# A four-layer fp32 block on one core: SBUF tensors placed on multiples of 256 bytes, the delta rule's gate columns used as weights, and its output's products with the state grouped

## What is computed

```python
beta = jax.nn.sigmoid(dn_b)                       # dn_b, dn_a: 4 + 4 columns of h @ w_in
g = -jnp.exp(dn_A_log) * jax.nn.softplus(dn_a + dn_dt_bias)
...
def step(state, inp):                             # 4 chunks of 64 tokens, 4 heads
    u_c, w_c, a_c, qd_c, kt_c, dl_c = inp
    v_new = u_c - jnp.einsum('bhck,bhkv->bhcv', w_c, state)
    o = jnp.einsum('bhck,bhkv->bhcv', qd_c, state) + jnp.einsum('bhcj,bhjv->bhcv', a_c, v_new)
    state = state * dl_c[..., None, None] + jnp.einsum('bhck,bhcv->bhkv', kt_c, v_new)
    return state, o
```

## Time and profile before

| | |
|---|---|
| median of the runs | 1903.18 us |
| lowest and highest | 1902.38, 1908.37 us |
| the profiled execution | 1908.99 us, its span 1907.2 us |
| TensorE's mean granted clock | 0.993 |
| busy: TensorE, VectorE, ScalarE, GpSimd | 99%, 65%, 50%, 16% of the span |

### The profile page before, as it was taken

How to read it: one execution, slowest core, us unless ns; L and a number is a source line. 1 busy time by engine, 2 the same in 40 slices (tenths; PEclk the granted TensorE clock), 3 DMA queues, 4 the chain that set the end, 5 groups by cost and what they waited for, 6 DMA issues and landing times.

```text
span 1907.2 us, 36402 instructions
## 1 busy us (share of the span) xinstructions
PE 1879.3 (99%) x15460; PEld 1791.1 (94%) x15460; DVE 1246.2 (65%) x1678; ACT 955.7 (50%) x1381; POOL 308.5 (16%) x176
## 2 busy tenths in 40 slices
PE   7999999999999999999999999999999999999998
PEld 7989998998899999999989999999999899999998
DVE  6884567665689545877658775577547684677643
ACT  5633456544563435564445445555534444556533
POOL 0050231000003203200002342320001352321000
PEclk9999999999999999999999999999999999999999
DMA  6443344655445323555565553355555663345553
GB/s 228 161 145 111 120 146 159 211 187 198 145 154 178 110 97 127 200 181 182 193 209 184 178 179 131 123 188 193 187 186 179 211 195 121 132 167 188 190 187 100
DMA packets 92161, 317.59 MB, mean 167 GB/s; under 512 B 11744, under 2 KB 12896, under 8 KB 91744
## 3 DMA queue, kind: packets, MB, share of 16 engines
q1 hardware_dynamic: 91424, 314.69, 48.9%
q10 hardware_dynamic: 576, 0.57, 0.1%
HBM read 304.99 MB, written 1.05 MB: 160 GB/s over the span
## 4 chain that ended last, share of the span: by engine, by line
PE 90%; DVE 7%; ACT 1%; DMA 1%; issue 1%; SPq 0%; DVEq 0%; ACTq 0%
PE bank L2001 89%; DVE wlo L1126 3%; DVE area L1126 2%; PE bank L2543 1%; DVE area L1132 1%; DMA raw<-in_weights 1%; DVE hl L1132 1%; DVE xT L1132 1%; ACT area L630 1%; ACT whi L636 0%; PE bank L2561 0%; PE bank L2220 0%; DVE area L1196 0%; DVE xT L1126 0%; DVE area L1645 0%
## 5 line engine op out<-in xcount | busy, mean ns | idle before, releaser
L1126 DVE TENSOR_TENSOR wlo<-raw,whi 128x1024 fp32r<-128x1024 f32 x518 | 659.9, 1289 | 399.1 <-ACT whi L636 398.6
L2001 PE MATMUL bank<-hh,whi 128*128 128x256 f32 x2928 | 835.3, 286 | 15.8 <-DVE wlo L1126 13.1
L2001 PE MATMUL bank<-hh,wlo 128*128 128x256 f32 x2928 | 818.6, 281 | 0.0
L2001 PE MATMUL bank<-hl,whi 128*128 128x256 f32 x2928 | 811.7, 281 | 0.0
L636 ACT CAST whi<-raw 128x1024 fp32r<-128x1024 f32 x572 | 589.0, 1046 | 412.3 <-PE bank L2001 361.2
L2001 PEld LDWEIGHTS bank<-hh,whi 128*128 128x128 f32 x2928 | 555.7, 190 | 30.0 <-DVE wlo L1126 14.7
L2001 PEld LDWEIGHTS bank<-hl,whi 128*128 128x128 f32 x2928 | 555.8, 191 | 1.9 <-issue 1.9
L2001 PEld LDWEIGHTS bank<-hh,wlo 128*128 128x128 f32 x2928 | 556.2, 190 | 0.0
L1781 POOL TENSOR_TENSOR area<-area 128x512 f32<-128x512 f32 (+4 forms) x86 | 137.4, 1604 | 559.3 <-ACT area L630 219.4
L1781 POOL TENSOR_TENSOR wlo<-raw,whi 128x1024 fp32r<-128x1024 f32 x54 | 134.0, 2483 | 426.3 <-ACT whi L636 426.3
L2001 PE MATMUL bank<-area 64*64 64x64 f32 (+7 forms) x1928 | 184.9, 268 | 0.7 <-DVE area L1196 0.7
(11 more groups left out here) (129 smaller groups left out, 1915.5 us busy)
## 6 DMA issues: line engine op xcount, KB each, us to landing
raw<-in_weights SPq DMA_DIRECT2D x572, 512.0 KB, 4.1
area<-area SPq DMA_DIRECT2D x96, 64.0 KB, 3.5
area<-area SPq DMA_DIRECT2D x16, 128.0 KB, 3.8
cst<-in_const SPq DMA_DIRECT2D x1, 1188.0 KB, 7.3
cst<-in_const SPq DMA_DIRECT2D x1, 1024.5 KB, 5.5
xT<-in_x SPq DMA_DIRECT2D x4, 256.0 KB, 8.0
out<-xT SPq DMA_DIRECT2D x4, 256.0 KB, 2.9
area<-in_lev SPq DMA_DIRECT2D x2, 384.0 KB, 6.6
```

Source lines behind the costliest of these rows:

```text
L1126: return v.tensor_tensor(dst, x, y, op)
L2001: return e.matmul(ps, x, y, start=start, stop=stop, skip_group_check=skip)
```

## The change

It does three things. It allocates hh, hl, RSB, the region of area, SW and cst in that order right after wlo, so that each starts on a multiple of 256 bytes; par, small and RST come last. It computes the gate columns with SW as weights (16 or 8 columns) and hh, hl as the moving operand, into 16 rows of a bank, one step earlier; VectorE copies these rows to ABR, and two fp32 matmuls with ABR as weights and a stacked 16 x 8 identity (8 new columns of `small`) as moving operand transpose them and add the high and the low half. ScalarE's cast of SW and VectorE's subtraction move to after the second step of qkv, ahead of the third; the bank of the result is freed by "ab". And the four products with the state are issued ahead of the four with v_new, the first of each bank with the start flag.

```diff
@@ -56,7 +56,7 @@
                          ("dnout", 1), ("retout", 4), ("pscale", 4), ("alog", 8), ("dtb", 8)])
 N_PAR2 = _columns(PAR2, [("attn", 8), ("mlp", 8), ("final", 8), ("idxk", 1), ("sinks", 8)])
 N_PAR = DEPTH * (N_PAR1 + N_PAR2)
-N_SMALL = 64 + 512
+N_SMALL = 64 + 512 + 8
 
 
 class Job:
@@ -319,17 +319,19 @@
         raw = sb("raw", [P, RAW, 1024])
         whi = sb("whi", [P, RING, 1024], F32R)
         wlo = sb("wlo", [P, RING, 1024], F32R)
+
+        hh = sb("hh", [P, 8, T], F32R)
+        hl = sb("hl", [P, 8, T], F32R)
+        RSB = sb("RSB", [P, T])
+        region = at[0]
+        assert region % 256 == 0, region
+        at[0] += 30 * 4096
+        SW = sb("SW", [P, 8, 16], F32R)
         cst = sb("cst", [P, N_CONST])
         par = sb("par", [P, N_PAR])
         small = sb("small", [P, N_SMALL])
         RST = sb("RST", [P, 2])
-        hh = sb("hh", [P, 8, T], F32R)
-        hl = sb("hl", [P, 8, T], F32R)
-        RSB = sb("RSB", [P, T])
-        SW = sb("SW", [P, 8, 16], F32R)
-        region = at[0]
-        nslots = (nc.sbuf_usable_end - region) // 4096
-        assert nslots >= 30, nslots
+        assert at[0] <= nc.sbuf_usable_end, at[0]
         area = nc.alloc_sbuf_tensor_at("area", [P, 30 * 1024], F32, offset=region)
 
         def slot(i, n=1):
@@ -396,8 +398,10 @@
         a_, be, g_, eg, kx = (SM[:, 16 * i:16 * i + 8] for i in (0, 1, 2, 4, 5))
         G_, GL = SM[:, 48:56], SM[:, 56:64]
         u1, u2 = SM[:, 128:136], SM[:, 144:152]
-        AB2, tmp2 = (SM[:, c:c + 16].rearrange("p (s c) -> p s c", s=2) for c in (192, 224))
+        AB2 = SM[:, 192:208].rearrange("p (s c) -> p s c", s=2)
         AB = SM[:, 192:208].rearrange("p (s c) -> p c s", s=2)
+
+        ABR = SM[0:16, 0:256]
         sm3 = small[:, 0:64].rearrange("p (k c) -> p k c", c=8)
 
         QF = slot(0, 7)
@@ -878,8 +882,6 @@
 
                 def hook():
                     factor(norm)
-                    a.wait_ge(s_small[L], 16)
-                    a.copy(SW[:, :, 0:8], sm3).then_inc(*a_dn.up("SW", L))
 
                 def rv(m0):
                     a.wait_ge(*v_norm.at("turned", norm))
@@ -888,6 +890,8 @@
                 qkv = project("qkv", L, conv, hook)
                 next(qkv)
                 next(qkv)
+                a.wait_ge(s_small[L], 16)
+                a.copy(SW[:, :, 0:8], sm3).then_inc(*a_dn.up("SW", L))
                 next(qkv)
                 next(qkv)
                 a.wait_ge(*v_dn.at("ab", L))
@@ -1438,22 +1442,19 @@
 
                 def hook():
                     factor(norm)
-                    v.wait_ge(*a_dn.at("SW", L))
-                    tt(SW[:, :, 8:16], sm3, SW[:, :, 0:8].bitcast(F32), OP.subtract).then_inc(*v_dn.up("SW", L))
+                    v.wait_ge(*e_dn.at("abrow", L))
+                    v.tensor_copy(ABR, bank[1][0:16, 0:256]).then_inc(*v_dn.up("abrow", L))
 
                 qkv = project("qkv", L, conv, hook, norm)
                 next(qkv)
                 next(qkv)
+                v.wait_ge(*a_dn.at("SW", L))
+                tt(SW[:, :, 8:16], sm3, SW[:, :, 0:8].bitcast(F32), OP.subtract).then_inc(*v_dn.up("SW", L))
                 next(qkv)
                 next(qkv)
-                two = bank[1][:, 0:32].rearrange("p (s c) -> p s c", s=2)
                 v.wait_ge(*e_dn.at("ab", L))
-                v.tensor_copy(tmp2, two[:, :, 8:16]).then_inc(*v_dn.up())
-                v.wait_ge(*v_dn.now())
-                tt(AB2, two[:, :, 0:8], tmp2, OP.add).then_inc(*v_dn.up("absum", L))
-                v.wait_ge(*v_dn.now())
                 v.wait_ge(*v_norm.at("turned", norm))
-                tt(AB2, AB2, wide(RST[:, :], 2, 8), OP.mult).then_inc(*v_dn.up("ab", L))
+                tt(AB2, bank[1][:, 256:272].rearrange("p (s c) -> p s c", s=2), wide(RST[:, :], 2, 8), OP.mult).then_inc(*v_dn.up("ab", L))
                 v.wait_ge(*v_dn.now())
 
                 dn = delta(L)
@@ -2348,12 +2349,17 @@
                     if n == 0:
                         e.wait_ge(*g_dn.at("q", L))
                         fresh2(2, lambda j: a_dn.at("OD", L, j))
+
+                    def place(h):
+                        return bank[2 + h // 2][:, 256 * (h % 2) + 64 * n:256 * (h % 2) + 64 * n + 64]
+
+
+                    if n:
+                        for h in range(4):
+                            mm(place(h), St[:, 128 * h:128 * h + 128], Aq[:, 256 * h + 64 * n:256 * h + 64 * n + 64], h % 2 == 0, False, True)
                     for h in range(4):
                         b = 2 * h + half
-                        o = bank[2 + h // 2][:, 256 * (h % 2) + 64 * n:256 * (h % 2) + 64 * n + 64]
-                        if n:
-                            mm(o, St[:, 128 * h:128 * h + 128], Aq[:, 256 * h + 64 * n:256 * h + 64 * n + 64], True, False)
-                        x = mm(o, hv(VN)[r, h, :], AT[r, 128 * b + 64 * q:128 * b + 64 * q + 64], n == 0, True)
+                        x = mm(place(h), hv(VN)[r, h, :], AT[r, 128 * b + 64 * q:128 * b + 64 * q + 64], n == 0, True, True)
                     x.then_inc(*e_dn.up("o", L, n))
                     yield 1
                 e.wait_ge(*a_dn.at("square", L))
@@ -2459,13 +2465,18 @@
                 next(qkv)
                 next(qkv)
                 next(qkv)
+
+                e.wait_ge(*v_dn.at("SW", L))
+                fresh(1, v_dn.at("ab", L))
+                for k in range(8):
+                    mm(bank[1][0:16, 0:T], SW[:, k, :], hh[:, k, :], k == 0, False, True)
+                    x = mm(bank[1][0:8, 0:T], SW[:, k, 0:8], hl[:, k, :], False, k == 7, True)
+                x.then_inc(*e_dn.up("abrow", L))
                 next(qkv)
-                e.wait_ge(*v_dn.at("SW", L))
-                fresh(1, v_dn.at("absum", L))
+
+                e.wait_ge(*v_dn.at("abrow", L))
                 for s in range(2):
-                    for k in range(8):
-                        mm(bank[1][:, 16 * s:16 * s + 16], hh[:, k, 128 * s:128 * s + 128], SW[:, k, :], k == 0, False, True)
-                        x = mm(bank[1][:, 16 * s:16 * s + 8], hl[:, k, 128 * s:128 * s + 128], SW[:, k, 0:8], False, k == 7, True)
+                    x = mm(bank[1][:, T + 8 * s:T + 8 * s + 8], ABR[:, 128 * s:128 * s + 128], small[0:16, 576:584], True, True)
                 x.then_inc(*e_dn.up("ab", L))
                 dn = delta(L)
                 next(dn)
@@ -2777,6 +2788,7 @@
         put(PAR2, par2, "sinks", x["sinks_2"][l].reshape(2, 2, 2).transpose(0, 2, 1).reshape(1, 8))
         small[l][:, 0:64] = x["w_in"][l][:, 2048:2056].reshape(8, P, 8).transpose(1, 0, 2).reshape(P, 64)
         small[l][:, 64:576] = x["pool_w"][l].transpose(1, 0, 2).reshape(P, 512)
+        small[l][0:16, 576:584] = np.tile(np.eye(8, dtype=np.float32), (2, 1))
     return par1, par2, small
 
 
```

## The result

| | before | after |
|---|---|---|
| median of the runs, us | 1905.78 (1902.38 to 1908.69, 4 runs) | 1932.31 (1930.33 to 1934.22, 4 runs) |
| profiled execution, us (span) | 1909.0 (1907.2) | 1931.89 (1930.1) |
| matmuls of 256 columns, start to start, mean ns | 116.0 | 119.9 |
| matmuls of 512 columns, the same | 230.2 | 227.1 |
| stretches at half clock between the clock's first rise (at 17.39 and at 12.15 us) and the last 6 us | 4 | none |

The ratio is 1.014 (1.012 to 1.016). The forecast was 1863, 1815 to 1898; the rival "slower", at 1924, had the sign and came nearest, and missed the time by 8 us.

What follows compares the result with a forecast made beforehand. TensorE, busy 99% of the span, was taken as the bound: matmul count times spacing. 33 + 1.8 + 5.2 + 5.1 = 45 us off 1909.0 gave 1864, from the median 1861; forecast 1863 us, range 1815 to 1898.

Steps and rivals of the forecast that it cites:

- rival "slower": 256-column matmuls whose moving operand starts on a multiple of 256 read worse: 2.6 ns each, 30 us, 1924 us; chance 0.13.
- What bounds the kernel: Whole kernel: TensorE, busy 99% of the span, so time is to first order matmul count times start-to-start spacing.
- Part 1, the layout: All fp32r matmuls: operands moved onto multiples of 256 bytes save 2.7 ns each, 33 us in all.
- between -6.4 ns and nothing: Limits set on the layout's gain per matmul: at most from the mean 0.1154 down to 0.109 us, at least no gain.
- decision point: Slower reading of moving operands outweighs the gains from gate columns and output order from 0.8 ns per matmul.
- rival "the layout is worth nothing": Operand addresses do not change matmul spacing, as 192 already sits on 16-byte lines; about 1894 us, chance 0.29.
- the floor: All matmul spacing falls to 0.109 us (0.218 for 512 columns), giving 1814 us; a rival with chance 0.14.
- Part 2, the gate columns: Gate columns with SW as weights: 1.2 to 1.6 us less per layer on TensorE, 1.8 us at the end, no clock falls there.
- TensorE's lead: Convolution: most of TensorE's gain is lost waiting for VectorE's 6.12 us loop; idle gaps grow from 0.1 to over 1 us.
- Part 3, the output: Output's state products issued first: 0.87 us less per chunk, 5.2 us in all, 24 passes in about 3.1 us.
- the clock: Output blocks: half-clock stretches of 6.83 and 3.42 us expected gone, saving half, 5.1 us; perhaps less in a median run.
- The sum: Whole kernel: 33 + 1.8 + 5.2 + 5.1 = 45 us less; forecast 1863 us, chance 0.42.

Runs made afterwards that it cites:

- the stream alone: Only the projections' fp32r matmuls on copies of the input, all else left out, over offsets of weights and moving operand; 113.3 to 120.0 ns per 256-column matmul, no kernel time.
- the three kernels above: All of the change, with hh at 192, distance 64, or distance +256: 1902.36, 1915.37 and 1933.66 us; each still had one 3.4 us fall of the clock.

## Why the prediction was wrong, by its steps

**What bounds the kernel: right.** Count times spacing moved the end: 46.0 us of slower spacing against 26.5 us in the medians; the edits, and waits and edges that shrink with a slower TensorE, lie between.

**Part 1, the layout (-33 us forecast): the sign was wrong, and this step alone sinks the forecast.** Undone by itself it was worth 30 us (1902.4 to 1932.3), and put in by itself it cost 32. The step that failed is the choice of value: "I take the difference that the neighbours show between an operand pair off and half on multiples, 0.1117 - 0.109 = 2.7 ns: it is the nearest row that changes an offset alone". It does not change an offset alone. The gate columns run through the distances 0, 64, 128 and 192 by turns, since SW's columns of each k start 64 bytes after the last, and move 8 or 16 columns; the transposes are another kind of instruction. Neither is near a stream of 256 columns at one distance. The bound "between -6.4 ns and nothing" left the loss out of the part, and the question was put wrongly before it: offset of each operand from a multiple, and not of one from the other. With the weights at 0 the two are the same in every 256-column row of the trace of before, so it could not be read there; weights at 64, and all at 192, separated them.

**The rival "slower": right in sign, with the wrong mechanism and too small a size.** It read the sign from the right place, the fixed loss of the 512-column stream against the 256-column one. Its price, 2.6 ns, was 3.9 by measurement (119.9 - 116.0), and 6.8 against the lower level from which it was worked out (119.9 - 113.1). Its decision point, 0.8 ns, was far exceeded. But its cause, "the start of the moving operand", is refuted by the kernel with moving at 0 and weights at 64, which ran at 114.5 ns and 1887 us. The objection made to it, "both levels occur with the same operands at the same addresses", was put to another rival and held there: distance 192 has two levels. But distance 0 has one, above both. With a chance of 0.13 the only rival that used fp32r rows of long streams was rated last.

**The rival "the layout is worth nothing": wrong.** The Trainium skill (SBUF — State Buffer, Specifications) gives lines of 16 bytes and says nothing there of how a start changes the rate; that the layout therefore changes nothing was the prediction's inference. The runs refute it: starts that are all multiples of 16 gave 113.3 to 120.0 ns. On the floor: the section that the prediction names (the Trainium skill, TensorE: Matmul & The Clock Gate, Back-to-back issue gap) gives columns / 2.4 + 2.5 ns for an isolated matmul, and says that in a stream of weight loads and matmuls both set the spacing; the prediction took it for the stream. The runs do not reach its 109.2 ns: no stretch of 256-column fp32r matmuls was under 113.3 in any run, over 64 pairs of places.

**Part 2, the gate columns (-1.8 us and the falls of the clock at 31.04 and 532.8): right in its rows, not resolved at the end, and half right on the clock.** The 16 matmuls took 1.9 us for 1.8, the transposes 0.61 for 0.6. Each took 0.118 us and not 0.113: their distances run through 0, 64, 128 and 192, and the stream alone has 120.0, 117.8, 118.7 and 113.3 or 117.8 there, a mean of 117.5 to 118.6; the stream had 128 weight columns and not 16 or 8, so this is a comparison and no proof. Behind layer 0's gate columns the clock fell in all three kernels with the old form (31.04, 30.80, 31.50 us) and in none of the eleven profiled executions with the new one. In layer 1 the prediction had the wrong source, or not the whole one: the fall went with the output's order alone, with the gate columns as they were. And TensorE's lead did go into VectorE's loop, as said; in after it waits where it did not in before. The forecast had gaps of over 1 us; at 119.9 ns the longest are 0.70 and, in layer 1, 0.86 us, and with hh at 192 (116.2 ns) 1.43 and 1.75 us:
```profile
41.74 0.39 PE L2002 MATMUL bank<-hh,whi 128*128 128x256 f32 x1 [0.70 <-DVE wlo L1130]
48.14 0.38 PE L2002 MATMUL bank<-hh,whi 128*128 128x256 f32 x1 [0.39 <-DVE wlo L1130]
```
VectorE's side of the same, the eviction that waited 0.76 us at 37.38 and the loop behind it:
```profile
35.19 0.68 DVE L1130 TENSOR_TENSOR area<-bank,RSB 128x512 f32<-128x512 f32 x1
...
46.86 2.36 DVE L1130 TENSOR_TENSOR wlo<-raw,whi 128x1024 fp32r<-128x1024 f32 x2 [0.30 <-ACT whi L640]
...
52.99 2.36 DVE L1130 TENSOR_TENSOR wlo<-raw,whi 128x1024 fp32r<-128x1024 f32 x2 [0.30 <-ACT whi L640]
```
The eviction no longer waits, the splits come 2.2 us earlier (46.86 for 49.08), 0.9 of it because the whole stage was earlier (the clock rose at 12.15 us of this execution and at 17.39 of before's, and with the same edits it has risen at either), and the loop itself is still 6.13 us: 1.3 us gained for 1.1 forecast. The end moved by 1.0 us or less between the kernels without and with this part, which their spread does not resolve.

**Part 3, the output: held for the products, in part by luck for the clock.** 24 passes take 3.22 us for "about 3.1", 0.84 less for 0.87. At distance 0 products and clock come to 5.0 + 5.1 us by count against 9.8 measured, for 5.2 + 5.1 forecast. The forecast had two falls of 6.83 and 3.42 us, and what went were three of 3.4, one of them the fall given to the gate columns. And the falls behind the output did not go everywhere, as the three kernels above show. With the operands of before, both edits together brought 6.4 us (1908.7 to 1902.4) and not the 12 of parts 2, 3 and the clock. The trace of that kernel shows what can account for the difference: 256 columns at 116.2 ns for 116.0 (some 3 us), 512 columns at 231.8 for 230.2 (1.6 us), and the fall at 671.18 (half of 3.4 us). It is one execution, and the runs spread by 15 us, so this is an account and no proof.

**The sum.** Without part 1 it is 1863 + 33 = 1896; the edits alone measured 1902.4, beside a kernel before that took 1908.7 there and not the 1903.2 on which the sum was made. The layout's 30 on top are 1932.

## What to carry to other kernels

Where TensorE is bound by a stream of short matmuls, measure start to start in two or three quiet stretches, and try where the moving operand starts relative to its weights: steps of 32 bytes moved each matmul by up to 6.7 ns of 120, for nothing but an offset in the allocator. Then time the whole kernel: distance 112, the best in the stream alone with weights at 0, ran near the slowest level with weights at 144. A rule like "put it on a multiple" can be the worst case of it: with all operands on multiples of 256 the distance is 0. Time each part of a change alone before they are joined, and look at the addresses of what stands behind a tensor that is made wider; here 6 to 11 us lay in the edits, and 30 against them in the layout.

## What the hardware showed that was not expected

- The spacing of fp32r matmuls with 128 x 128 weights and 256 moving columns depends on (start of moving - start of weights) modulo 256: 120.0 ns at 0 and 96, 118.7 at 128, 117.8 at 64, 113.3 or 117.8 at 192. The kernel's spacing at 0, 64, 128, 192 and 224 is there, within 0.4 ns, with all other engines idle too. This holds for starts on multiples of 32 bytes. Why is open; no run here separates the reading of the weights from that of the moving operand.
- At 192, and at 32 and 160, a stretch takes one of two levels and holds it until the stream is interrupted: none of the 59 unbroken stretches of 24 matmuls or more in before changes its level. The same pair took either one in following blocks, but the list of sixteen distances run a second time gave every block the level of the first time, so what picks it repeats; what it is was not found. The kernel before and the two with the edits at distance 192 differ by it: 116.0 and 116.2 with weights at 0, 114.5 with weights at 64, though in the stream alone neither pair was the better.
- Distance 112 is the best with weights at 0, 64 and 128 (113.3 to some 114.5) and as bad as distance 0 with weights at 16 or 144 (120.0). At distances other than 112, places 16 past a multiple of 32 were tried only for the moving operand, with weights at 0.
- For 512 columns the order is another: 227 to 228 ns at distance 0, 229 to 232 at 64, 233 at 32, 144 and 192.
